# A decoder step on one core: in six key slots ScalarE sums two pages over the heads and VectorE two instead of three

## Chip, core and metric

One NeuronCore of a Trainium2 chip runs the whole program in one launch. The metric is the device time of one execution in microseconds (us). A core has TensorE (PE), VectorE (DVE), ScalarE (ACT), GpSimd (POOL) and SyncE (SP), each with an instruction stream of its own, and they meet only through semaphores. SyncE does no arithmetic here: it issues nearly all transfers.

## What is computed

One layer of a decoder for 256 prompt rows and 8 sample rows of 1024 columns, in float32. Only the sample rows' attention is touched. Each of the 8 samples has 2048 past tokens, which lie in 16 pages of 128 tokens in a key pool and a value pool:

```python
z = x @ w_in                                    # q | k | v | B | C | h
s = jnp.einsum('bthd,bthnd->bthn', q, k_g) / math.sqrt(HEAD_DIM) - slope * dist
p = jax.nn.softmax(where(valid, s, -inf))       # valid: the top 3 blocks of 256 tokens, and the own one
att = jnp.einsum('bthn,bthnd->bthd', p, v_g)
mix = concat([att, gb * conv(gc * h)]) @ w_out
x1 = layer_norm(ALPHA * x + mix)                # then a gated FFN with a convolution, and a second norm
```

A score is the dot product of a key and the query over the 64 columns of each of 8 heads.

## The kernel before

**Key slots.** The 8 x 16 key pages are worked through in 32 slots of four pages (1 MB), numbered j from 0. Slot j uses buffer j % 4 of the tile KV (in the trace also "qk<-KV,qk" for its products). For each slot the pages are multiplied by the sample's broadcast query into one of two product buffers, `prod[:, j % 2]`, and the products are then summed over the 64 columns of each head into the tile T:

- VectorE multiplies all four pages (`multiply`, L939, 128x2048), or three of them (128x1536) in the slots of `POOLED`, where GpSimd multiplies the fourth (`multiply_page`, L560).
- VectorE sums the first three pages (`reduce`, L949, 1536 products to 24 sums), or all four in the slots of `WHOLE`.
- ScalarE sums the fourth page (`sum_products`, L669): eight copies of 64 columns, each followed by a read of the accumulator.

VectorE multiplies slot j + 1 ahead of the sum of slot j. `multiply(j)` writes over the products of slot j - 2, so it waits until these have been summed: always for VectorE's sum (`s_red`), and for ScalarE's (`s_reda`) only where VectorE itself writes the fourth page.

**Other work in the same streams.** The order on each engine is written out by hand. Between about 100 and 126 us TensorE makes the last projection tiles (`z_tile`, L1437) and the prompt attention's transposes and outputs; ScalarE copies them out of PSUM (`z_tile`, L674, into zbuf; `head_transposes`, L704, into hT; `head_out`, L708, into catT). In ScalarE's order slot 19's sum stands after `head_transposes(2)` and ahead of `z_tile(22)`, `kv_rows(5)`, `head_out(0)`, `head_out(1)` and `head_transposes(3)`. GpSimd gates the convolution's four slices with a product each (L590), with two page products among them, and then does the samples' columns in one small product (L591):

```python
for t in range(4):
    if t >= 2:
        multiply_page(18 + t)
    pool.wait_ge(s_ze, 20 + t + 1)
    nc.gpsimd.tensor_tensor(catT[:, 4 + t, 0:NPR], catT[:, 4 + t, 0:NPR], zT[:, 12 + t, 0:NPR], ALU.mult).then_inc(s_cvT, 1)
nc.gpsimd.tensor_tensor(catT[:, 4:8, NPR:R], cus, zT[:, 12:16, NPR:R], ALU.mult).then_inc(s_cvT, 1)
```

TensorE then waits for all five of these (`s_cvT`) ahead of `values(0, 0)`, L1608, the first product of probabilities with values. From there it runs `values` and `mix_tile` (L1632, L1634) in turn. VectorE's `residual(m)` (L1060) follows each mix tile, between the key slots.

**Transfers.** SyncE issues the loads of keys and values in one fixed sequence (`load_keys`, `load_values`; L360 is the line that both issue from). `load_keys` waits for the product of the slot that last used the buffer. `load_values` waits for the product of TensorE that last read its buffer; that is so from the fourth value load on.

Of the kernel before, what the change touches and what calls it, by code (L numbers as in the profile page):

```python
# [16 lines left out]
ACT = mybir.ActivationFunctionType  # L17
# [11 lines left out]
NH, DH = 8, 64  # L29
DA = NH * DH  # L30
# [10 lines left out]
GP = 4  # L41
SLOTS = NPAGE // GP
GD = GP - 1
# [8 lines left out]
NL = FT - E  # L52
WHOLE = (14, 16, 18, 20, 31)
POOLED = (9, 10, 11, 12) + tuple(range(17, 32))
FIRST_SAMPLES = FT - 4
WARM = 14
HOMES = (6, 4, 5, 6, 4, 5, 6, 4, 5) + tuple((0, 4, 1, 5, 2, 3)[v % 6] for v in range(23))
# [2 lines left out]
def build(nc, x_prompt, x_sample, cache_k, cache_v, state_conv, state_ffn_conv, page_table,  # L60
# [13 lines left out]
    with ctx:  # L74
        def sb(name, shape, dt=F32):
            return ctx.enter_context(nc.sbuf_tensor(name, shape, dt))[:]
# [9 lines left out]
        def sem(name):  # L86
            return ctx.enter_context(nc.semaphore(name))
# [44 lines left out]
        T = sb("T", [P, 2, NPAGE + 1, 4 * NH])  # L132
# [41 lines left out]
        prod = qk[:, 1, :].rearrange("p (u n) -> p u n", u=2)  # L174
# [63 lines left out]
        s_kused, s_vused = sem("k_slot_used"), sem("v_slot_used")  # L238
        s_kpool = sem("k_page_used_pool")
# [91 lines left out]
        def act_sums(j):  # L331
            return sum(i not in WHOLE for i in range(j))

        def pool_pages(j):
            return sum(i in POOLED for i in range(j))

# [7 lines left out]
        def _(sp):  # L344
# [43 lines left out]
            def load_keys(b, s, ids):  # L388
                sp.wait_ge(s_kused, b * SLOTS + (s + 1 - SLOTS))
                if b * SLOTS + s - SLOTS in POOLED:  # L390
                    sp.wait_ge(s_kpool, pool_pages(b * SLOTS + (s + 1 - SLOTS)))
# [132 lines left out]
        def _(pool):  # L524
# [91 lines left out]
            def split_f(u, src):  # L616
                pool.wait_ge(s_f, u + 1)
                nc.gpsimd.tensor_copy(fh[:, u, 0:NPR], src).then_inc(s_fh, 1)
                pool.wait_ge(s_fh, u + 1)
                nc.gpsimd.tensor_tensor(fl[:, u, 0:NPR], src, fh[:, u, 0:NPR], ALU.subtract).then_inc(s_fs, 1)  # L620

            def split_samples(first, end):
                pool.wait_ge(s_sf, 1)
                chain(nc.gpsimd.tensor_copy(fh[:, first:end, NPR:R], sf[:, first:end, :]))
                nc.gpsimd.tensor_tensor(fl[:, first:end, NPR:R], sf[:, first:end, :], fh[:, first:end, NPR:R],
                                        ALU.subtract).then_inc(s_fss, 1)
# [4 lines left out]
            for v in range(NL - 1):  # L631
                split_f(E + v, ftmp[:, v % 2, :])
                if v == FIRST_SAMPLES - E:
                    split_samples(0, FIRST_SAMPLES)
            pool.wait_ge(s_var2, 1)
# [8 lines left out]
        def _(act):  # L644
# [14 lines left out]
            def sum_products(j):  # L659
                b, s = divmod(j, SLOTS)  # L660
                if j in WHOLE:
                    return
                if j in POOLED:
                    act.wait_ge(s_kpool, pool_pages(j + 1))
                else:
                    act.wait_ge(s_kused, j + 1)
                for h in range(NH):
                    x = prod[:, j % 2, GD * DA + h * DH:GD * DA + (h + 1) * DH]
                    ins = nc.scalar.activation(x, x, ACT.Copy, accum_out=T[:, b // 4, GP * s + GD, b % 4 * NH + h:b % 4 * NH + h + 1])  # L669
                ins.then_inc(s_reda, 1)  # L670

            def z_tile(n):
# [51 lines left out]
            load_win(1)  # L724
            query(1)
            sum_products(0)
            for j in range(1, 4):
                z_tile(j - 1)
                query(2 * j)
                query(2 * j + 1)  # L730
                sum_products(j)
# [8 lines left out]
            for j in range(4, 8):  # L740
                sum_products(j)
                z_tile(j)
# [88 lines left out]
            def silu(u):  # L831
                act.wait_ge(s_cv, 2 * u + 1)
                nc.scalar.activation(U[:, u % 2, 0, :], U[:, u % 2, 0, :], ACT.Silu).then_inc(s_si, 1)
# [31 lines left out]
            def late_scaled(v):  # L865
                u = E + v
                for a in range(2):
                    act.wait_ge(s_u, 2 * u + a + 1)
                    act.wait_ge(s_f, u - 1)
                    bank = ps[:, 2 * late_slot(v) + a, :]  # L870
                    nc.scalar.activation(U[:, u % 2, a, :], bank[:, 0:NPR], ACT.Copy, scale=tap(u + a * FT, 2))
                    nc.scalar.activation(uptail[:, :, u + a * FT], bank[:, TAIL:R], ACT.Copy).then_inc(s_tl, 1)

            for v in range(NL - 1):
# [6 lines left out]
                if v >= 1:  # L881
                    silu(E + v - 1)
                if v == FIRST_SAMPLES - E + 1:
                    act.wait_ge(s_sv, 1)
                    nc.scalar.activation(sf[:, 0:FIRST_SAMPLES, :], cs2[:, 0:FIRST_SAMPLES, :], ACT.Silu).then_inc(s_si8, 1)
            late_scaled(NL - 1)
# [3 lines left out]
            act.wait_ge(s_sv, 2)  # L890
            nc.scalar.activation(sf[:, FIRST_SAMPLES:FT, :], cs2[:, FIRST_SAMPLES:FT, :], ACT.Silu).then_inc(s_si8, 1)
            act.wait_ge(s_f, FT)
            act.wait_ge(s_sf, 2)
            act.wait_ge(s_fss, 3)
            for c in range(3):
                act.wait_ge(s_utps, c + 1)
                n = min(4, NTAIL - 4 * c)
# [9 lines left out]
        def _(dve):  # L907
# [21 lines left out]
            def multiply(j):  # L929
                b, s = divmod(j, SLOTS)  # L930
                dve.wait_ge(s_qb, b + 1)
                dve.wait_ge(s_kv[s], 16 * GP * b + 16 * GP)
                if j >= 2:
                    dve.wait_ge(s_red, j - 1)
                    if j not in POOLED:
                        dve.wait_ge(s_reda, act_sums(j - 1))
                n = GD if j in POOLED else GP
                q = qb[:, b:b + 1, :].to_broadcast([P, n, DA])
                nc.vector.tensor_tensor(prod[:, j % 2, 0:n * DA].rearrange("p (g d) -> p g d", g=n), kv[:, s, 0:n], q,  # L939
                                        ALU.mult).then_inc(s_kused, 1)  # L940

            def reduce(j):
                b, s = divmod(j, SLOTS)
                n = GP if j in WHOLE else GD
                dve.wait_ge(s_kused, j + 1)
                if j in WHOLE and j in POOLED:
                    dve.wait_ge(s_kpool, pool_pages(j + 1))
                dst = T[:, b // 4, GP * s:GP * s + n, b % 4 * NH:(b % 4 + 1) * NH]
                nc.vector.tensor_reduce(dst, prod[:, j % 2, 0:n * DA].rearrange("p (g h d) -> p g h d", h=NH, d=DH),  # L949
                                        AX.X, ALU.add).then_inc(s_red, 1)  # L950

            def scan(j):
                if j + 1 < NS * SLOTS:
                    multiply(j + 1)
                reduce(j)
# [102 lines left out]
            def residual(m):  # L1058
                dve.wait_ge(s_mix, m + 1)
                nc.vector.scalar_tensor_tensor(rT[:, m, :], xT[:, m, :], ALPHA, ps[:, mix_bank(m), 0:R], ALU.mult, ALU.add)\  # L1060
                    .then_inc(s_r1, 1)

            multiply(0)
            for j in range(8):
                scan(j)
# [24 lines left out]
            scan(15)  # L1090
            head_reciprocals(2)
            multiply(17)
            reduce(16)
            gate_penalties(0)
            head_masked(3)
            multiply(18)
            token_max(0)
            max_diagonal(0)
            reduce(17)
            head_reciprocals(3)  # L1100
            shifted_scores(0)
# [41 lines left out]
            _, x, _, out = first_rows[1]  # L1143
# [113 lines left out]
            for a in range(2):  # L1257
                src = ps[:, 7, :].rearrange("p (n a x) -> p a n x", a=2, x=32)
                ins = nc.vector.tensor_copy(tails[:, a, 0:E, :], src[:, a, 0:E, 0:NS])
            ins.then_inc(s_ett, 1)  # L1260

            def late_convolved(v):
                u, s = E + v, late_slot(v)
                if v < NL - 1:
                    convolved(u, ps[:, 2 * s, 0:NPR], ps[:, 2 * s + 1, 0:NPR])
                    return
                for a in range(2):
                    for k in (1, 0):
                        n = NPR - 2 + k
                        if k:  # L1270
                            dve.wait_ge(s_tl, E + 2 * v + a + 1)
                        else:
                            dve.wait_ge(s_c1, 2 * u + a + 1)
                        out = U[:, u % 2, a, 2 - k:NPR]
                        nc.vector.scalar_tensor_tensor(out, ps[:, 2 * s + a, 0:n], tap(u + a * FT, k), out, ALU.mult, ALU.add)\
                            .then_inc(s_c1 if k else s_cv, 1)
# [17 lines left out]
            for v in range(NL):  # L1294
# [6 lines left out]
                late_convolved(v)  # L1301
                if v == FIRST_SAMPLES - E:
                    dve.wait_ge(s_cst, 1)
# [67 lines left out]
            n, _, _, out = row_tiles[2]  # L1371
# [563 lines left out]
```

## Time and profile before

| what | value |
|---|---|
| median of 3 runs | 438.06 us (437.49 to 438.96) |
| profiled execution | 437.8 us, of which 436.0 us span |
| TensorE busy | 412.7 us, 95% |
| VectorE busy | 294.7 us, 68% |
| ScalarE busy | 181.4 us, 42% |
| GpSimd busy | 110.8 us, 25% |
| moved by DMA | 124.60 MB, mean 286 GB/s |

The span is what the profiler saw between the first and the last instruction; the rest of the 437.8 us lies around it. A share of busy time is a mean over stages with different limits: the key slots end at about 183 us, and from 262 us on the FFN's products keep TensorE busy with little else.

### The profile page before, as it was taken

What the parts mean: (1) busy time and instruction counts of PE and PEld (TensorE: products, weight loads), DVE (VectorE), ACT (ScalarE), POOL (GpSimd) and SP (SyncE); (2) the same over time, 40 slices, a digit from 0 to 9 for tenths busy, and PEclk for the clock granted to TensorE, in tenths of its full rate; (3) what the DMA queues carried; (4) which work ended last, traced back from release to release, by engine and by line L of the source; (5) the groups of instructions that cost most, each with busy time, mean ns of one, the idle gap of its engine ahead of it and who ended that gap; (6) DMA issues with size and microseconds to landing.
All of it is one profiled execution on the core that took longest, in us unless ns stands there. A gap on an engine that the chain in (4) does not pass through costs nothing.

```text
span 436.0 us, 8237 instructions
## 1 busy us (share of the span) xinstructions
PE 412.7 (95%) x2903; PEld 339.2 (78%) x2903; DVE 294.7 (68%) x382; ACT 181.4 (42%) x694; POOL 110.8 (25%) x133
## 2 busy tenths in 40 slices
PE   4999999999999998999999989999999999999990
PEld 4588887876876774765653479999999999999990
DVE  0498999999799976954541275666776776534437
ACT  1587569644469133112110243554455555233201
POOL 1005334995255152200000717122211220000002
PEclk9999999999999999999999999999999999999997
DMA  8999999899999999999999953665556766676002
GB/s 313 397 359 407 405 407 393 316 404 409 409 359 327 338 404 405 406 405 404 402 405 398 318 196 98 194 191 162 158 169 191 213 181 186 183 211 206 3 2 99
DMA packets 109515, 124.60 MB, mean 286 GB/s; under 512 B 5903, under 2 KB 67048, under 8 KB 109466
## 3 DMA queue, kind: packets, MB, share of 16 engines
q1 hardware_dynamic: 101138, 107.30, 70.2%
q10 hardware_dynamic: 8336, 16.78, 10.2%
q8 instruction: 23, 0.38, 0.3%
q14 instruction: 18, 0.15, 0.1%
HBM read 121.65 MB, written 2.61 MB: 285 GB/s over the span
## 4 chain that ended last, share of the span: by engine, by line
PE 64%; DVE 18%; DMA 5%; issue 5%; SPq 4%; POOL 2%; ACT 1%; DVEq 0%; POOLq 0%; ACTq 0%
PE ps L1821 12%; PE ps L1822 11%; PE ps L1823 11%; PE ps L1714 8%; PE ps L1608 6%; DVE qk L939 6%; DVE T L949 5%; PE ps L1437 4%; PE ps L1632 4%; PE ps L1634 3%; PE ps L1384 3%; SPq L360 2%; DMA wring<-in_cache_v 2%; DMA KV<-in_cache_k 2%; POOL x1l L612 1%
## 5 line engine op out<-in xcount | busy, mean ns | idle before, releaser
L1188 DVE TENSOR_TENSOR wlo<-KV,whi 128x2048 fp32r<-128x2048 f32 (+1 forms) x24 | 61.7, 2571 | 57.5 <-ACT whi L838 29.3
L1437 PE MATMUL ps<-xT,wring 128*128 128x264 f32 x384 | 89.6, 388 | 0.1
L1437 PEld LDWEIGHTS ps<-xT,wring 128*128 128x128 f32 x384 | 71.6, 190 | 13.6 <-issue 1.7
L1821 PE MATMUL ps<-x1h,whi 128*128 128x264 f32 x256 | 73.7, 288 | 0.2
L1822 PE MATMUL ps<-x1l,whi 128*128 128x264 f32 x256 | 72.7, 284 | 0.0
L1823 PE MATMUL ps<-x1h,wlo 128*128 128x264 f32 x256 | 72.6, 284 | 0.0
L939 DVE TENSOR_TENSOR qk<-KV,qk 128x1536 f32<-128x1536 f32 (+1 forms) x32 | 67.0, 2097 | 6.6 <-DMA KV<-in_cache_k 2.7
L669 ACT ACTIVATE qk<-qk 128x64 f32<-128x64 f32 x216 | 51.9, 245 | 29.1 <-POOL qk L560 23.1
L949 DVE TENSOR_REDUCE T<-qk 128x24 f32<-128x1536 f32 (+1 forms) x32 | 58.4, 1827 | 0.0
L1821 PE MATMUL ps<-fh,whi 128*128 128x264 f32 x176 | 50.4, 286 | 0.1
L1822 PE MATMUL ps<-fl,whi 128*128 128x264 f32 x176 | 50.0, 284 | 0.0
L1823 PE MATMUL ps<-fh,wlo 128*128 128x264 f32 x176 | 49.9, 284 | 0.0
L1821 PEld LDWEIGHTS ps<-x1h,whi 128*128 128x128 f32 x256 | 48.2, 188 | 1.7 <-issue 1.3
L838 ACT ACTIVATE whi<-KV 128x2048 fp32r<-128x2048 f32 x16 | 30.7, 1916 | 42.4 <-PE ps L1823 42.4
L1822 PEld LDWEIGHTS ps<-x1l,whi 128*128 128x128 f32 x256 | 48.3, 188 | 0.0
L1823 PEld LDWEIGHTS ps<-x1h,wlo 128*128 128x128 f32 x256 | 48.1, 188 | 0.0
L560 POOL TENSOR_TENSOR qk<-KV,qk 128x512 f32<-128x512 f32 x19 | 33.3, 1758 | 37.9 <-DMA KV<-in_cache_k 23.7
L669 ACT ACTIVATION_READ_ACCUMULATOR qk<-qk 128x1 f32 x216 | 41.0, 190 | 0.0
L1168 DVE SCALAR_TENSOR_TENSOR U<-ps,stT,U 128x255 f32<-128x255 f32 (+1 forms) x84 | 34.5, 474 | 0.0
L1821 PEld LDWEIGHTS ps<-fh,whi 128*128 128x128 f32 x176 | 33.2, 188 | 0.6 <-DVE wlo L1188 0.5
L1822 PEld LDWEIGHTS ps<-fl,whi 128*128 128x128 f32 x176 | 33.2, 188 | 0.0
L1823 PEld LDWEIGHTS ps<-fh,wlo 128*128 128x128 f32 x176 | 33.1, 188 | 0.0
(215 smaller groups left out, 574.0 us busy)
## 6 DMA issues: line engine op xcount, KB each, us to landing
KV<-in_cache_k SPq DMA_DIRECT2D x128, 256.0 KB, 6.2
KV<-in_w_ffn_up SPq DMA_DIRECT2D x32, 512.0 KB, 4.7
KV<-in_cache_v SPq DMA_DIRECT2D x60, 256.0 KB, 7.3
wring<-in_cache_v SPq DMA_DIRECT2D x56, 256.0 KB, 6.4
KV<-in_w_ffn_down SPq DMA_DIRECT2D x8, 1408.0 KB, 6.3
wring<-in_w_in ACTq DMA_DIRECT2D x5, 2048.0 KB, 14.0
zbuf<-in_cache_v SPq DMA_DIRECT2D x12, 256.0 KB, 5.3
zbuf<-in_w_ffn_up SPq DMA_DIRECT2D x3, 1024.0 KB, 10.2
```

The costliest lines, as they stand in the source:

```text
L560: nc.gpsimd.tensor_tensor(prod[:, j % 2, GD * DA:GP * DA], kv[:, s, GD, :], qb[:, b, :], ALU.mult).then_inc(s_kpool, 1)
L669: ins = nc.scalar.activation(x, x, ACT.Copy, accum_out=T[:, b // 4, GP * s + GD, b % 4 * NH + h:b % 4 * NH + h + 1])
L838: nc.scalar.activation(whi[s][:, 0:UNIT], w2[s][:, 0:UNIT], ACT.Copy).then_inc(s_hi, 1)
L939: nc.vector.tensor_tensor(prod[:, j % 2, 0:n * DA].rearrange("p (g d) -> p g d", g=n), kv[:, s, 0:n], q, ALU.mult).then_inc(s_kused, 1)
L949: nc.vector.tensor_reduce(dst, prod[:, j % 2, 0:n * DA].rearrange("p (g h d) -> p g h d", h=NH, d=DH), AX.X, ALU.add).then_inc(s_red, 1)
L1168: nc.vector.scalar_tensor_tensor(out, bank[:, 0:n], tap(u + a * FT, k), out, ALU.mult, ALU.add)\
L1188: nc.vector.tensor_tensor(wlo[s][:, 0:n], w2[s][:, 0:n], whi[s][:, 0:n], ALU.subtract).then_inc(s_lo, 1)
L1437: ins = nc.tensor.matmul(ps[:, z_bank(n), 0:R], tile[k], xT[:, k, :], start=k == 0, stop=k == KT - 1)
L1714: ins = nc.tensor.matmul(ps[:, u % 4, a * NPR:(a + 1) * NPR], early(u, k, a), x1T[:, k, 0:NPR], start=k == 0, stop=k == KT - 1)
L1821: nc.tensor.matmul(out, wh[k], xh[k], start=k == 0, stop=False)
L1822: nc.tensor.matmul(out, wh[k], xl[k], start=False, stop=False)
L1823: ins = nc.tensor.matmul(out, wl[k], xh[k], start=False, stop=k == n - 1)
```

## The change

In the six slots of a new table `HALVED`, `reduce` sums two pages on VectorE (1024 products to 16 sums) in place of three. `sum_products` sums the third page as well as the fourth on ScalarE: sixteen copies in place of eight. The third page's part waits for VectorE's product and the fourth's for GpSimd's. Since ScalarE now reads products that VectorE wrote, `multiply(j)` on VectorE waits for ScalarE's sums where slot j - 2 is in the table.

```diff
+HALVED = (17, 19, 22, 24, 26, 28)
...
-                if j in POOLED:
-                    act.wait_ge(s_kpool, pool_pages(j + 1))
-                else:
-                    act.wait_ge(s_kused, j + 1)
-                for h in range(NH):
-                    x = prod[:, j % 2, GD * DA + h * DH:GD * DA + (h + 1) * DH]
-                    ins = nc.scalar.activation(x, x, ACT.Copy, accum_out=T[:, b // 4, GP * s + GD, b % 4 * NH + h:b % 4 * NH + h + 1])
+                for g in range(2 if j in HALVED else GD, GP):
+                    if g == GD and j in POOLED:
+                        act.wait_ge(s_kpool, pool_pages(j + 1))
+                    else:
+                        act.wait_ge(s_kused, j + 1)
+                    for h in range(NH):
+                        x = prod[:, j % 2, g * DA + h * DH:g * DA + (h + 1) * DH]
+                        ins = nc.scalar.activation(x, x, ACT.Copy, accum_out=T[:, b // 4, GP * s + g, b % 4 * NH + h:b % 4 * NH + h + 1])
...
-                    if j not in POOLED:
+                    if j not in POOLED or j - 2 in HALVED:
                         dve.wait_ge(s_reda, act_sums(j - 1))
...
-                n = GP if j in WHOLE else GD
+                n = GP if j in WHOLE else 2 if j in HALVED else GD
```

ScalarE's stream around slot 19's sum, before (hT and hT_53 are the prompt attention's transposes, zbuf the projection, catT the outputs):

```order
L681 ACTIVATE rows<-ps 128x512
L704 ACTIVATE hT<-ps 128x384 x2
L669 ACTIVATE qk,T<-qk 128x64 x8
L674 ACTIVATE zbuf<-ps 128x264
L683 ACTIVATE srows<-ps 8x512
L708 ACTIVATE catT<-ps 128x256 x2
L704 ACTIVATE hT_53<-ps 128x384 x2
L674 ACTIVATE zbuf<-ps 128x264
L708 ACTIVATE catT<-ps 128x256 x2
L803 ACTIVATE ctail<-ps 10x512
```

The same place of the changed kernel, whose lines stand two lower:

```order
L683 ACTIVATE rows<-ps 128x512
L706 ACTIVATE hT<-ps 128x384 x2
L671 ACTIVATE qk,T<-qk 128x64 x16
L676 ACTIVATE zbuf<-ps 128x264
L685 ACTIVATE srows<-ps 8x512
L710 ACTIVATE catT<-ps 128x256 x2
L706 ACTIVATE hT_53<-ps 128x384 x2
L676 ACTIVATE zbuf<-ps 128x264
L710 ACTIVATE catT<-ps 128x256 x2
L805 ACTIVATE ctail<-ps 10x512
```

Eight copies more stand ahead of everything that ScalarE does from `z_tile(22)` on.

VectorE's stream from the product of slot 20 to that of slot 22, before (Pw, ownp and vsT belong to the samples' softmax):

```order
L939 TENSOR_TENSOR qk<-KV,qk 128x1536 [waits scores_summed_dve,k_landed0,q_broadcast]
L949 TENSOR_REDUCE T<-qk 128x3x8 [waits k_slot_used]
L1036 TENSOR_TENSOR ownp<-T,rden 64x4x4 [waits sample_values_copied]
L1038 TENSOR_TENSOR ownp<-ownp,vsT 128x4x4 [waits own_weights]
L939 TENSOR_TENSOR qk<-KV,qk 128x1536 [waits k_landed1,scores_summed_dve,q_broadcast,dve_chain]
L949 TENSOR_REDUCE T<-qk 128x4x8 [waits k_page_used_pool,k_slot_used]
L939 TENSOR_TENSOR qk<-KV,qk 128x1536 [waits scores_summed_dve,k_landed2,q_broadcast]
```

And of the changed kernel:

```order
L941 TENSOR_TENSOR qk<-KV,qk 128x1536 [waits scores_summed_dve,k_landed0,q_broadcast]
L951 TENSOR_REDUCE T<-qk 128x2x8 [waits k_slot_used]
L1038 TENSOR_TENSOR ownp<-T,rden 64x4x4 [waits sample_values_copied]
L1040 TENSOR_TENSOR ownp<-ownp,vsT 128x4x4 [waits own_weights]
L941 TENSOR_TENSOR qk<-KV,qk 128x1536 [waits scores_summed_dve,k_landed1,scores_summed_act,q_broadcast,dve_chain]
L951 TENSOR_REDUCE T<-qk 128x4x8 [waits k_page_used_pool,k_slot_used]
L941 TENSOR_TENSOR qk<-KV,qk 128x1536 [waits scores_summed_dve,k_landed2,q_broadcast]
```

Slot 19's sum is a page shorter, and slot 21's product waits for `scores_summed_act`, which it did not.

## Rows read from the trace of the kernel before

**Rows 1.** Busy time by engine in three stretches, with DMA share and rate

```profile
125.00:150.00 25.00, 24.43 (x136) 16.78 (x132) 24.73 (x18) 15.18 (x115) 10.98 (x8) 1.00 0.95 323
150.00:226.00 76.00, 74.28 (x458) 47.01 (x450) 47.64 (x82) 16.63 (x72) 10.21 (x5) 1.00 1.05 404
226.00:237.00 11.00, 9.67 (x62) 4.93 (x66) 2.08 (x3) 0.00 (x0) 0.00 (x0) 1.00 1.05 403
```

**Rows 2.** Waits of SyncE's queue, 100 to 170 us: total, times, longest

```profile
SPq L360 <- DVE qk L939: 6.8, 3, 3.2
SPq L360 <- PE ps L1608: 2.2, 1, 2.2
```

**Rows 3.** TensorE's timeline: start, us, [idle before <- releaser]

```profile
126.27 0.60 PE L1384 MATMUL ps<-ident,zbuf 128*10 128x128 f32 x4 [0.57 <-ACT catT L708]
126.80 1.06 PE L1608 MATMUL ps<-zbuf,Pw 128*32 128x512 f32 x8
...
226.37 1.07 PE L1608 MATMUL ps<-KV,Pw 128*32 128x512 f32 x8 [0.45 <-DMA KV<-in_cache_v]
...
234.12 1.06 PE L1608 MATMUL ps<-KV,Pw 128*32 128x512 f32 x8 [0.80 <-DMA KV<-in_cache_v]
...
236.70 1.07 PE L1608 MATMUL ps<-wring,Pw 128*32 128x512 f32 x8 [0.17 <-DMA wring<-in_cache_v]
```

**Rows 4.** ScalarE's timeline around the sums of slots 17, 19 and 27

```profile
101.43 0.26 ACT L669 ACTIVATE qk<-qk 128x64 f32<-128x64 f32 x1 [5.75 <-POOL qk L560]
...
119.59 0.26 ACT L669 ACTIVATE qk<-qk 128x64 f32<-128x64 f32 x1
...
121.41 0.19 ACT L669 ACTIVATION_READ_ACCUMULATOR qk<-qk 128x1 f32 x1
121.50 0.37 ACT L674 ACTIVATE zbuf<-ps 128x264 f32<-128x264 f32 x1
...
122.78 0.83 ACT L704 ACTIVATE hT<-ps 128x384 f32<-128x384 f32 x2
...
125.74 0.38 ACT L708 ACTIVATE catT<-ps 128x256 f32<-128x256 f32 x1 [0.27 <-PE ps L1488]
...
147.97 0.26 ACT L669 ACTIVATE qk<-qk 128x64 f32<-128x64 f32 x1 [6.38 <-POOL qk L560]
```

**Rows 5.** VectorE's timeline: slots 19 to 22, and the last residual

```profile
120.02 1.75 DVE L949 TENSOR_REDUCE T<-qk 128x24 f32<-128x1536 f32 x1
...
122.75 2.77 DVE L939 TENSOR_TENSOR qk<-KV,qk 128x1536 f32<-128x1536 f32 x1
125.44 2.27 DVE L949 TENSOR_REDUCE T<-qk 128x32 f32<-128x2048 f32 x1
127.85 1.76 DVE L939 TENSOR_TENSOR qk<-KV,qk 128x1536 f32<-128x1536 f32 x1
...
164.29 0.43 DVE L1060 SCALAR_TENSOR_TENSOR xT<-xT,ps 128x264 f32<-128x264 f32 x1 [2.10 <-PE ps L1634]
```

**Rows 6.** GpSimd's timeline at the same place

```profile
121.95 0.73 POOL L590 TENSOR_TENSOR catT<-catT,zbuf 128x256 f32<-128x256 f32 x1 [5.29 <-ACT zbuf L674]
122.64 1.27 POOL L560 TENSOR_TENSOR qk<-KV,qk 128x512 f32<-128x512 f32 x1
124.70 1.40 POOL L590 TENSOR_TENSOR catT<-catT,zbuf 128x256 f32<-128x256 f32 x1 [0.80 <-ACT zbuf L674]
126.07 0.25 POOL L591 TENSOR_TENSOR catT<-cu,zbuf 128x32 f32<-128x32 f32 x1
```

**Rows 7.** GpSimd's timeline at 262 us

```profile
262.62 0.73 POOL L620 TENSOR_TENSOR fl<-qk,fh 128x256 fp32r<-128x256 f32 x1
263.30 2.46 POOL L618 CAST fh<-qk 128x256 fp32r<-128x256 f32 x1
...
266.52 0.40 POOL L618 CAST fh<-qk 128x256 fp32r<-128x256 f32 x1
```

**Rows 8.** VectorE's timeline at 263 us

```profile
263.08 2.42 DVE L1188 TENSOR_TENSOR wlo<-KV,whi 128x2048 fp32r<-128x2048 f32 x1 [3.53 <-ACT whi L838]
```

## Prediction

> **What bounds the kernel now.** I first cut the span into stretches. From 125 to 150 us VectorE is busy 24.73 of 25 us, and TensorE 24.43; the transfers run at 323 GB/s. From 150 to 226 us they run at 404 GB/s, and at 403 from there to 237 us, which I take as full; TensorE is still busy 74.28 of 76 us [rows 1]. So two things are full at once: TensorE, and later the transfers. Between 125 and 150 us the transfers could have carried a quarter more: 25 us x (1 - 323/404) = 5.0 us of their time is lost there. Whoever gives buffers back sooner in that stretch may shift all that follows.
>
> Who does? In the waits of SyncE's queue, VectorE's product holds it three times for 6.8 us in total, TensorE's `values` once for 2.2 us [rows 2]. VectorE's longest, 3.2 us, is for slot 20's product; in VectorE's order that product stands behind a softmax step which itself waits for a projection tile of TensorE. After 130 us the queue's one wait of any size is that for `values`, since from the fourth value load on a value page can only be fetched when TensorE has read the one before it.
>
> TensorE's timeline shows what it lacks. At 126.27 us it has waited 0.57 us for ScalarE's copy of catT, at 126.80 us `values(0, 0)` begins. At the end of the value loads it waits for transfers three times, 0.45 + 0.80 + 0.17 = 1.42 us [rows 3]. Nothing in between waits for VectorE's key slots: at 164.29 us the last `residual` has itself waited 2.10 us for TensorE [rows 5]. VectorE is full from 125 to 150 us, but is ahead of those who need it.
>
> **What VectorE saves.** A sum of three pages takes 1.75 us, one of four 2.27 us [rows 5], 0.52 us a page. Two pages cost some 1.23 us by that. Six slots save 6 x 0.52 = 3.1 us of VectorE. I cost this at nothing on the path: slot 17's saving goes into waits for ScalarE's exponentials and for TensorE, slot 19's into the wait below, and those of 22 to 28 into the 2.10 us at 164 us and what was ahead of it.
>
> **What ScalarE gets.** Eight copies with their reads took 121.50 - 119.59 = 1.91 us [rows 4]. Six slots add 11.5 us to ScalarE. In most this is hidden: slot 17's fourth page comes after a wait of 5.75 us for GpSimd, slot 27's after 6.38 us [rows 4], and the third page's products are there long before, so that it is summed inside such a wait; the slots around have ones of the same kind or, at 22 and 24, a backlog of one page against a cycle of two slots on VectorE of 8 us. Without that cover each would cost its 1.91 us.
>
> **Slot 19 is different.** Its sum begins at 119.59 us, straight behind `head_transposes(2)`, and ScalarE goes on at 121.50 us without a gap [rows 4]. There is no wait to hide in. All behind it comes 1.91 us later until ScalarE's next idle time. Step by step:
>
> 1. Slot 19's last read ended at 121.41 + 0.19 = 121.60 us and now ends at 123.51. The copy of tile 22 ended at 121.50 + 0.37 = 121.87 and now ends at 123.78.
> 2. `multiply(21)` on VectorE, which began at 122.75 us [rows 5], now waits for slot 19. It begins at about 123.65 us. Before, it took 2.77 us in place of the 1.76 us of slot 22's [rows 5], since GpSimd had begun a product at 122.64 that lasted to 123.91 [rows 6]: it ended 1.61 us after that. Now it is alone and ends at 123.65 + 1.76 = 125.4 us, as before. Queued behind it are VectorE's sum of 20 and the slots after, which so lose nothing.
> 3. GpSimd's gating of slice 2 waits for tile 22 and began at 121.95, 0.08 us after the copy [rows 6]; now at 123.86 us. That is 0.2 us after `multiply(21)` began, and the two don't run at once: the gating at 124.70 us took 1.40 us in place of 0.73, and ended 0.58 us after VectorE's product of 122.75 to 125.52 [rows 5, 6]. So slice 2 ends at 125.4 + 0.6 = 126.0 us, page 21's product (1.27 us) at 127.25, slice 3 (0.73 us) at 127.95.
> 4. VectorE's sum of 20 (2.27 us, which doesn't hinder GpSimd) ends at 127.6, and `multiply(22)` is issued 0.14 us later as before [rows 5], at 127.75 us: while slice 3 is under way, and ahead of GpSimd's last small product, L591. What happens then is seen at 263 us: VectorE's product was issued at 263.08 during a GpSimd product that ended at 263.35; GpSimd's next, issued at 263.30, took 2.46 us in place of 0.40, to 265.76, and VectorE's ended at 265.50 [rows 7, 8]. VectorE goes in between. So `multiply(22)` runs from 127.95 for 1.61 us to 129.55, and L591 ends at about 129.7 us. It ended at 126.07 + 0.25 = 126.32 us [rows 6].
> 5. `values(0, 0)` waits for it. It began at 126.80 us [rows 3] and now begins at 129.75 us: 2.95 us later. By ScalarE's copies alone (its second pair of hT copies ends at 122.78 + 0.83 + 1.91 = 125.5, the last copy of catT moves from 125.74 to about 126.6 us) [rows 4] it would be 0.85 us.
>
> The page "SBUF — State Buffer" of the Trainium skill, section "Who interferes with whom", says that a VectorE instruction with two SBUF inputs and a GpSimd one that reads SBUF exclude each other, that issue order decides, and that `tensor_reduce` never contends; the trace agrees in all three. By it step 4 comes out as written.
>
> **From there to the end.** TensorE has a fixed order and no idle time until 165 us that could take this up. At 226 to 237 us, 1.42 us of waiting for transfers could: if the transfers came no later, TensorE would lose only 2.95 - 1.42 = 1.53 us. But they do come later. SyncE stands at `load_values(4)` until `values(0, 1)` is done [rows 2], the later value loads follow the same rule, and from 150 us on the transfers are full, so a pause of theirs is never made good. With all of it passed on the cost is 2.95 us. The pause need not grow by as much as TensorE's delay, since key loads between are not held by TensorE; I take 2.6 us, nearer the upper bound, as the stretch of 323 GB/s shows that little is queued there. Behind 237 us all follows TensorE at a fixed distance.
>
> Sum: 437.8 - 0 + 2.6 = 440.4 us for the profiled execution. This one lies 0.26 us under the median of the runs shown, so 440.5 us stands between the two. About 0.3%, 1.3 us, is what a measurement of this kernel can tell from no change.
>
> **Rivals.**
>
> - *L591 slips through.* If `multiply(22)` is issued 0.2 us later against GpSimd than I have it, L591 goes first and `values(0, 0)` begins at 128.2 us: 1.4 us late, and 438.8 to 439.4 us at the end. The margin of step 4 is only those 0.2 us, which speaks for it; that L591 is as late if `multiply(22)` comes earlier speaks against it.
> - *Hidden.* The delay at 126.8 us is only the 0.85 us of ScalarE's copies, or the transfers don't shift, and the 1.42 us take up most of it: 437.7 to 438.6 us. For it: a wait of the right size exists. Against it: the gating on GpSimd hangs on the same copy, and the loads on the same `values`.
> - *Faster.* VectorE's 3.1 us give key buffers back sooner, the 5.0 us of lost transfer time shrink, and TensorE's 1.42 us of waiting go: 437.8 - 1.4 = 436.4 us. It decides from where slot 19's extra 1.91 us is hidden and VectorE sets the releases. For it: 24.73 of 25 us busy and 6.8 us of SyncE's waits. Against it: after 130 us SyncE waits for TensorE. More than 1.4 us it can't be, as TensorE's own order is then the bound. The Trainium skill's page "Perfetto Trace Analysis", section "Optimizing Scalar/DVE Operations", speaks for this one: with VectorE saturated, moving work to ScalarE may make sense. The trace has the saturation, at 24.73 of 25 us, but not the dependence on it.
> - *Worse.* GpSimd's later pages push the key loads of 21 and 22 too, and the pause grows past 2.95 us: 441.3 to 443 us.
>
> **How the numbers follow.** Full collision 0.50 (439.6 to 441.3 us), L591 slipping through 0.20, hidden 0.15, faster 0.10, worse 0.05. The time is the first case's. The range from 438.0 to 441.5 us leaves out the faster case, part of the hidden one and the worse one. Slower by over 0.3% begins at 439.4 us: the first, the worst, and some of the second, less what the untested 0.2 us takes from my trust in the first: 0.60. Faster 0.10, the same 0.30. The first case's own range is 439.6 to 441.3 us.
>
> **What would show it.** In the changed kernel's trace ScalarE's copy of tile 22 ends near 123.8 us; `multiply(21)` begins near 123.65 us behind an idle time that ScalarE ended; GpSimd's gating of slice 2 lasts to 126.0 us; L591 ends near 129.7 us (128.2 us for the first rival, below 127 us for the hidden case), and `values(0, 0)` follows it at once. The load behind `values(0, 1)` is 2.95 us later. VectorE's two-page sums take 1.2 us each. The prediction is wrong if L591 isn't the last of the five that TensorE waits for, if SyncE's loads from 137 to 150 us don't move with `values`, or if two-page sums let the key loads at 130 us start sooner.

## The result and the profile after

The changed kernel takes 443.16 us (median of 4 runs, 442.0 to 443.76) against 437.84 us for the kernel before: a ratio of 1.0114, 95% interval 1.009 to 1.0138, or 5.0 us slower by the ratio. The range of the prediction ended at 441.5 us. The direction was right, the size was not.

The profiled execution took 442.0 us with a span of 440.2 us, 4.2 us more than that of the kernel before. Its lines stand two lower (one on GpSimd). Part of it only began later: the first matmul of the softmax gate, which both kernels make behind the same work, starts at 99.67 us before and at 100.31 us after. That start differs from execution to execution: in the two profiles below of the kernel before with one move or one delay it is at 100.46 and 100.06 us, and nothing ahead of it was changed there. TensorE's timeline, of the kernel before:

```profile
99.67 0.49 PE L1511 MATMUL ps<-alibir,identr 128*128 128x512 f32 x1 [0.86 <-DVE penx L998]
...
127.79 2.05 PE L1632 MATMUL ps<-catT,wring 128*128 128x264 f32 x8
...
135.00 1.07 PE L1608 MATMUL ps<-wring,Pw 128*32 128x512 f32 x8
```

and of the changed one, from there on, in which `values(0, 0)` is the product at 130.47 us:

```profile
100.31 0.49 PE L1513 MATMUL ps<-alibir,identr 128*128 128x512 f32 x1 [0.86 <-DVE penx L1000]
...
127.69 0.60 PE L1386 MATMUL ps<-ident,zbuf 128*10 128x128 f32 x4 [0.61 <-ACT catT L710]
130.47 1.94 PE L1610 MATMUL ps<-zbuf,Pw 128*32 128x512 f32 x8 [2.18 <-issue]
132.33 2.77 PE L1634 MATMUL ps<-catT,wring 128*128 128x264 f32 x8
...
140.26 1.07 PE L1610 MATMUL ps<-wring,Pw 128*32 128x512 f32 x8
...
238.29 1.07 PE L1610 MATMUL ps<-KV,Pw 128*32 128x512 f32 x8 [0.53 <-DMA KV<-in_cache_v]
```

I measure everything from that gate matmul. `values(0, 0)` comes 130.47 - 100.31 = 30.16 us behind it, before 126.80 - 99.67 = 27.13 us: 3.03 us later. `values(0, 1)`, at 140.26 us after and at 135.00 us before, comes 39.95 us behind it instead of 35.33: 4.62 us later. So 1.59 us more are lost between two products that have only TensorE's own work between them. `values(0, 0)` takes 1.94 us where it took 1.06 [rows 3], and the product of `mix_tile` behind it 2.77 us where it took 2.05: these two are the whole 1.6 us. At 140.26 us `values` takes 1.07 us again. The windows of the changed kernel show why (the number behind the busy times is the granted clock, then DMA share and GB/s):

```profile
126.00:130.00 4.00, 1.65 (x16) 0.79 (x12) 3.87 (x3) 2.74 (x15) 4.00 (x4) 1.00 0.98 341
130.00:131.00 1.00, 0.53 (x4) 0.23 (x8) 1.00 (x2) 1.00 (x11) 1.00 (x2) 0.71 0.92 326
131.00:132.00 1.00, 1.00 (x8) 0.00 (x0) 0.87 (x2) 1.00 (x10) 1.00 (x2) 0.50 0.93 338
...
133.00:134.00 1.00, 1.00 (x4) 0.79 (x3) 1.00 (x1) 1.00 (x10) 0.00 (x0) 0.59 0.25 78
134.00:135.00 1.00, 1.00 (x6) 0.84 (x6) 1.00 (x2) 1.00 (x10) 0.19 (x1) 1.00 0.94 320
```

The granted clock is 1.00 until 130 us, 0.50 from 131 to beyond 133 us, and 1.00 again from 134 us: TensorE falls from 2.4 to 1.2 GHz at the end of its 2.18 us of idle time.

The first stretch of [rows 1], after. TensorE's busy time from 125 to 150 us is 2.5 us less, part of it spent at the low clock, and the transfers lose more of their time, 275 against 323 GB/s:

```profile
125.00:150.00 25.00, 21.89 (x113) 14.65 (x117) 21.73 (x16) 18.92 (x144) 11.55 (x9) 0.93 0.81 275
```

SyncE's queue, as in [rows 2]: VectorE holds it for 6.7 us as before, TensorE's `values` for 6.9 us where it was 2.2. The largest holder in both lists is GpSimd's page product, 7.1 us before and 7.7 after, which [rows 2] and the prediction leave out.

```profile
SPq L361 <- PE ps L1610: 6.9, 3, 3.8
SPq L361 <- DVE qk L941: 6.7, 3, 3.4
```

ScalarE, as in [rows 4]: slot 17's fourth page still waits for GpSimd (3.69 us in place of 5.75, the rest is now the third page's sum); slot 19's sixteen copies run without a gap from 120.23 us, and tile 22 is copied at 124.05 us.

```profile
102.07 0.26 ACT L671 ACTIVATE qk<-qk 128x64 f32<-128x64 f32 x1 [3.69 <-POOL qk L561]
...
120.23 0.26 ACT L671 ACTIVATE qk<-qk 128x64 f32<-128x64 f32 x1
...
124.05 0.38 ACT L676 ACTIVATE zbuf<-ps 128x264 f32<-128x264 f32 x1
...
127.17 0.38 ACT L710 ACTIVATE catT<-ps 128x256 f32<-128x256 f32 x1 [0.48 <-PE ps L1490]
```

VectorE, as in [rows 5]:

```profile
120.66 1.21 DVE L951 TENSOR_REDUCE T<-qk 128x16 f32<-128x1024 f32 x1
...
124.28 1.76 DVE L941 TENSOR_TENSOR qk<-KV,qk 128x1536 f32<-128x1536 f32 x1 [1.90 <-ACT qk L671]
...
128.37 1.78 DVE L941 TENSOR_TENSOR qk<-KV,qk 128x1536 f32<-128x1536 f32 x1
```

GpSimd, as in [rows 6]. The last row is the samples' small product: 1.76 us in place of 0.25. The first is slice 2, which meets VectorE's product at 124.28 us and takes 2.13 us in place of 0.73.

```profile
124.50 2.13 POOL L591 TENSOR_TENSOR catT<-catT,zbuf 128x256 f32<-128x256 f32 x1 [7.20 <-ACT zbuf L676]
126.59 1.26 POOL L561 TENSOR_TENSOR qk<-KV,qk 128x512 f32<-128x512 f32 x1
127.82 0.71 POOL L591 TENSOR_TENSOR catT<-catT,zbuf 128x256 f32<-128x256 f32 x1
128.50 1.76 POOL L592 TENSOR_TENSOR catT<-cu,zbuf 128x32 f32<-128x32 f32 x1
```

VectorE's sums by form (busy, mean ns): 1744 - 1208 = 536 ns are saved in each of six slots, 3.2 us.

```profile
L951 DVE TENSOR_REDUCE T<-qk 128x24 f32<-128x1536 f32 x21 | 36.6, 1744 | 0.0
...
L951 DVE TENSOR_REDUCE T<-qk 128x16 f32<-128x1024 f32 x6 | 7.2, 1208 | 0.0
```

### The profile page after: what moved, and what is told of

Same layout as the page of the kernel before. It is cut to its first block, busy times and chain, and to the rows that moved or that the text cites. A ratio compares the mean times of both kernels' runs of the same rounds, so it can differ in the third digit from the quotient of the medians.

```text
span 440.2 us, 8338 instructions
## 1 busy us (share of the span) xinstructions
PE 414.5 (94%) x2903; PEld 340.2 (77%) x2903; DVE 290.5 (66%) x382; ACT 192.6 (44%) x790; POOL 111.1 (25%) x133
## 4 chain that ended last, share of the span: by engine, by line
PE 50%; DVE 17%; SPq 11%; issue 10%; DMA 6%; POOL 3%; ACT 2%; DVEq 0%; POOLq 0%; ACTq 0%
PE ps L1823 11%; PE ps L1824 11%; PE ps L1825 11%; SPq L361 9%; DVE qk L941 5%; DVE T L951 5%; PE ps L1716 4%; PE ps L1439 3%; DMA KV<-in_cache_k 3%; PE ps L1610 2%; PE ps L1386 2%; DMA wring<-in_cache_v 2%; POOL x1l L613 1%; PE ps L1802 1%; DVE wlo L1190 1%
## 5 line engine op out<-in xcount | busy, mean ns | idle before, releaser
L941 DVE TENSOR_TENSOR qk<-KV,qk 128x1536 f32<-128x1536 f32 (+1 forms) x32 | 66.0, 2065 | 11.1 <-DMA KV<-in_cache_k 4.3
L671 ACT ACTIVATE qk<-qk 128x64 f32<-128x64 f32 x264 | 63.3, 244 | 22.6 <-DVE qk L941 13.1
L951 DVE TENSOR_REDUCE T<-qk 128x24 f32<-128x1536 f32 (+2 forms) x32 | 55.2, 1727 | 0.0
L671 ACT ACTIVATION_READ_ACCUMULATOR qk<-qk 128x1 f32 x264 | 50.1, 190 | 0.0
L561 POOL TENSOR_TENSOR qk<-KV,qk 128x512 f32<-128x512 f32 x19 | 31.5, 1660 | 37.9 <-ACT qk L671 18.4
L845 ACT ACTIVATE whi<-KV 128x2816 fp32r<-128x2816 f32 x8 | 20.5, 2558 | 29.8 <-PE ps L1825 29.8
```

Source lines behind the costliest of these rows:

```text
L561: nc.gpsimd.tensor_tensor(prod[:, j % 2, GD * DA:GP * DA], kv[:, s, GD, :], qb[:, b, :], ALU.mult).then_inc(s_kpool, 1)
```

## The experiments

Theory A: slot 19 alone does the harm. Its extra ScalarE work makes GpSimd's small product collide with VectorE's product of slot 22, TensorE waits for it, and its clock drops around that wait. Theory B, the rival: more ScalarE work and VectorE's new waits cost something in every slot.

"Late" below is how much later than in the kernel before `values(0, 0)` and `values(0, 1)` come behind the gate's first matmul, in the profile. The difference in us is the ratio less one, times 437.5 us.

| kernel | late, (0, 0) and (0, 1) | median us | ratio and interval | difference |
|---|---|---|---|---|
| changed kernel | 3.03, 4.62 | 443.16 | 1.0114 (1.009 to 1.0138) | 5.0 |
| without slot 19 | -0.02, -0.01 | 437.56 | 1.0003 (0.999 to 1.0015) | 0.1 |
| slot 19 alone | 3.03, 4.68 | 442.78 | 1.0119 (1.0099 to 1.0138) | 5.2 |
| page 21 last | 0.80, 0.81 | 438.16 | 1.0014 (1.0004 to 1.0024) | 0.6 |
| two idle matmuls | 2.87, 2.87 | 440.32 | 1.0064 (1.0045 to 1.0084) | 2.8 |
| sum 19 early | -0.01, 0.00 | 437.84 | 0.9996 (0.9986 to 1.0006) | -0.2 |
| before, sum 19 early | -0.01, -0.01 | 437.30 | 0.9996 (0.9984 to 1.0008) | -0.2 |
| before, ScalarE delayed | 1.71, 1.72 | 439.16 | 1.0034 (1.0021 to 1.0046) | 1.5 |
| slot 22 waits | 1.51, 1.51 | 439.14 | 1.0031 (1.0019 to 1.0043) | 1.4 |
| one idle matmul | 2.87, 2.88 | 440.78 | 1.0083 (1.007 to 1.0096) | 3.6 |
| changed kernel again | 3.03, 5.95 | 442.65 | 1.0114 (1.0097 to 1.013) | 5.0 |

**Which slots.** One run leaves slot 19 out of the table, the other keeps only it.

```diff
-HALVED = (17, 19, 22, 24, 26, 28)
+HALVED = (17, 22, 24, 26, 28)
```

> The table without slot 19: (17, 22, 24, 26, 28). Theory A (slot 19's extra 1.91 us of ScalarE is the whole cause: it makes GpSimd's small product L592 miss VectorE's product of slot 22, TensorE idles 2.2 us and then works for a while at the lower clock): within 0.5 us of the kernel before, 437.4 to 438.4 us, granted clock 1.00 from 125 to 150 us, values(0, 0) at about 126.8 us after the start of the span. Theory B (the extra ScalarE work and VectorE's new waits in all six slots each cost a share): five sixths of the loss stays, 441.5 to 442.5 us.

```diff
-HALVED = (17, 19, 22, 24, 26, 28)
+HALVED = (19,)
```

> The table with slot 19 alone. Theory A: the whole loss, 442 to 443.5 us. Theory B: one sixth of it, 438.3 to 439.2 us.

Without slot 19 the time is that of the kernel before, to 0.15%; with it alone the whole loss is there. Theory B falls. It also shows that the five other slots bring nothing: 2.7 us less work for VectorE, 9.6 us more for ScalarE, no change in the time.

The profile with slot 19 alone shows the fall of the clock a third time:

```profile
130.65 1.70 PE L1610 MATMUL ps<-zbuf,Pw 128*32 128x512 f32 x8 [2.18 <-issue]
```

```profile
130.00:131.00 1.00, 0.35 (x4) 0.19 (x8) 1.00 (x2) 1.00 (x9) 1.00 (x2) 0.97 0.86 320
131.00:132.00 1.00, 1.00 (x8) 0.00 (x0) 0.99 (x1) 0.30 (x3) 1.00 (x2) 0.50 1.03 231
```

The mean of 0.97 from 130 to 131 us puts the fall at about 130.94 us, some 0.3 us after `values(0, 0)` began and so just behind the idle time of 2.18 us, not in it.

**The collision.** GpSimd's page 21 is moved behind the gating:

```diff
-                if t >= 2:
-                    multiply_page(18 + t)
+                if t == 2:
+                    multiply_page(20)
...
+            multiply_page(21)
             multiply_page(22)
```

> The changed kernel, with GpSimd's product of page 21 moved behind the gating of slice 3 and the samples' product. Theory A: these two are done near 127.6 us, before VectorE's product of slot 22 is issued; TensorE waits only for ScalarE's copies and starts values(0, 0) about 1.0 us later than in the kernel before instead of 3.0; no fall of the granted clock: 438.5 to 439.3 us. If the collision with slot 22's product were not what holds the last product, it would stay at 442 to 443.5 us.

GpSimd's and TensorE's timelines of this run:

```profile
124.71 2.81 POOL L591 TENSOR_TENSOR catT<-catT,zbuf 128x256 f32<-128x256 f32 x2 [7.22 <-ACT zbuf L677]
127.48 0.25 POOL L592 TENSOR_TENSOR catT<-cu,zbuf 128x32 f32<-128x32 f32 x1
```

```profile
128.44 1.06 PE L1611 MATMUL ps<-zbuf,Pw 128*32 128x512 f32 x8
```

Slices 2 and 3 run in turn, the small product takes its 0.25 us again, and `values(0, 0)` is 0.80 us late. It follows the product before it without a wait, so this is ScalarE's copies alone. The run was expected 1.0 us late and at 438.5 us or more; it is a little faster. The other way round, GpSimd's order is kept and VectorE's product of slot 22 is made to wait:

```diff
                 dve.wait_ge(s_kv[s], 16 * GP * b + 16 * GP)
+                if j == 22:
+                    dve.wait_ge(s_cvT, 5)
                 if j >= 2:
```

> The changed kernel, with VectorE's product of slot 22 made to wait for the convolution's five products, so that GpSimd's last small product cannot be shut out. It takes 0.3 us of VectorE. Theory A: L592 takes 0.25 us in place of 1.76, values(0, 0) comes 1.5 us sooner than in the changed kernel, TensorE idles 0.6 us, the granted clock stays at 1.00: 439.0 to 440.0 us. If GpSimd's last product is slow for another reason: 442 to 443.5 us as without it.

```profile
127.92 0.72 POOL L591 TENSOR_TENSOR catT<-catT,zbuf 128x256 f32<-128x256 f32 x1
128.60 0.24 POOL L592 TENSOR_TENSOR catT<-cu,zbuf 128x32 f32<-128x32 f32 x1
```

```profile
129.05 1.06 PE L1612 MATMUL ps<-zbuf,Pw 128*32 128x512 f32 x8 [0.65 <-issue]
```

Only VectorE's product is out of the way, and the small product is back at 0.24 us. So the collision is shown from both sides, and it costs 1.5 us of the 3.0. The small product still ends at 128.84 us, shortly ahead of `values(0, 0)`: 0.7 us of the 1.51 are GpSimd's own, beyond the 0.80 of the copies.

**Delay or new wait.** Here the kernel before gets the delay on ScalarE and nothing of the rest:

```diff
             sum_products(19)
+            spare = ftmp.rearrange("p u n -> p (u n)")
+            sums = stats.rearrange("p r c s -> p (r c s)")
+            for h in range(NH):
+                nc.scalar.activation(spare[:, h * DH:(h + 1) * DH], slope[:, h:h + 1].to_broadcast([P, DH]), ACT.Copy,
+                                     accum_out=sums[:, h:h + 1])
```

> The kernel before, all its sums as they were, with eight copies of 128x64 with accumulator behind slot 19's sum that nobody needs. It gives ScalarE's delay of 1.91 us alone, without VectorE's new wait for slot 19: its product of slot 21 starts at 122.8 us and not at 123.7. Theory A: the collision happens all the same, 0.9 us sooner: L591 ends near 128.8 us, values(0, 0) is 2.0 us late, TensorE idles 1.1 us; 439.3 to 440.0 us if the granted clock holds, 441 to 441.7 us if it falls. If the new wait were the cause: within 0.5 us of the kernel before.

GpSimd's, VectorE's and TensorE's timelines:

```profile
124.24 0.79 POOL L590 TENSOR_TENSOR catT<-catT,zbuf 128x256 f32<-128x256 f32 x1 [7.21 <-ACT zbuf L674]
...
126.25 0.72 POOL L590 TENSOR_TENSOR catT<-catT,zbuf 128x256 f32<-128x256 f32 x1
126.93 1.76 POOL L591 TENSOR_TENSOR catT<-cu,zbuf 128x32 f32<-128x32 f32 x1
```

```profile
122.69 1.76 DVE L944 TENSOR_TENSOR qk<-KV,qk 128x1536 f32<-128x1536 f32 x1
...
126.77 1.81 DVE L944 TENSOR_TENSOR qk<-KV,qk 128x1536 f32<-128x1536 f32 x1
```

```profile
128.90 1.06 PE L1613 MATMUL ps<-zbuf,Pw 128*32 128x512 f32 x8 [0.86 <-issue]
```

The product of slot 21 starts unhindered at 122.69 us, that of slot 22 at 126.77 us, again while slice 3 is under way, and the small product is shut out for 1.76 us just the same. ScalarE's delay is enough for this collision. It gives 1.71 us of the 3.03. The other 1.3 us are a second collision: here slice 2 takes 0.79 us, in the changed kernel 2.13, as VectorE's product of slot 21 has waited for ScalarE there and starts just ahead of it. All of GpSimd's work behind slice 2 comes 1.34 us later by that. The shares of the two collisions depend on which is taken away first (1.5 and 0.7 us, or 0.9 and 1.3), as TensorE waits for whichever of the small product and the catT copies ends last. The run was expected at 2.0 us late and 439.3 us or more, and came out a little under both. The granted clock is 1.00 throughout 125 to 150 us here.

**The clock.** TensorE gets something to do while it waits: `keep_clock(5, 512)` is a matmul of 512 columns whose result nobody reads. None of the work that TensorE waits for comes sooner by that.

```diff
+            pe.wait_ge(s_soft, 1)
+            keep_clock(5, 512)
+            keep_clock(5, 512)
             pe.wait_ge(s_cvT, 5)
```

> The changed kernel, with two idle matmuls of 128x512 on TensorE (about 1 us each) ahead of the wait for the convolution's products, into the 2.2 us in which it idles. Nothing else is sooner. Theory A: the granted clock stays at 1.00, values(0, 0) is as late as in the changed kernel, and the 1.6 us that the low clock took from 130 to 134 us come back: 441.0 to 441.8 us. If the clock's fall does not come from the idle time, or costs nothing: 442.5 to 443.5 us as without it.

```profile
128.28 1.88 PE L1652 MATMUL ps<-ident 128*128 128x512 f32 x4
130.47 1.06 PE L1610 MATMUL ps<-zbuf,Pw 128*32 128x512 f32 x8 [0.30 <-POOL catT L592]
```

`values(0, 0)` is nearly as late as in the changed kernel (2.87 us against 3.03), but takes 1.06 us, and `values(0, 1)` is no later than it: the 1.6 us don't arise. The difference to the kernel before shrinks from 5.0 to 2.8 us, by 2.2 us and not by the 1.6 us of the first profile; the run is faster than the 441.0 us at which its expectation began. Two more runs bear on that. One takes a single `keep_clock` in place of two:

> The changed kernel with one idle matmul of 128x512 (1 us) ahead of the wait in place of two, so that TensorE idles about 1.2 us there. Theory A with the clock falling only for the whole idle time of 2.2 us: as with two, 440.0 to 440.8 us, granted clock 1.00 from 125 to 150 us. If any idle time above about a microsecond at this place drops the clock: 442 to 443.3 us.

```profile
127.99 1.02 PE L1652 MATMUL ps<-ident 128*128 128x512 f32 x2
130.18 1.06 PE L1610 MATMUL ps<-zbuf,Pw 128*32 128x512 f32 x8 [1.17 <-POOL catT L592]
```

TensorE idles 1.17 us, `values(0, 0)` takes 1.06 us and is no later than with two. The run is 0.8 us slower than that one, but the two intervals overlap. Nothing points to a fall of the clock in its other executions: their mean granted clocks are 0.991 to 0.994, and those of the kernel before 0.990 to 0.994. The other run is the changed kernel itself:

> The changed kernel once more, for a second profile and more times beside those of the kernel before on one chip. Theory A: values(0, 0) 3.0 us later after the gate's penalties than before (30.2 against 27.1 us), the granted clock at 0.50 for some 3 us behind it, 442.3 to 443.3 us. If the 5.3 us between the medians had more than these two parts (3.0 and 1.6 us), this profile would show where.

TensorE's timeline and the windows of this second profile, whose execution took 444.51 us:

```profile
100.00 0.49 PE L1513 MATMUL ps<-alibir,identr 128*128 128x512 f32 x1 [0.86 <-DVE penx L1000]
130.16 1.93 PE L1610 MATMUL ps<-zbuf,Pw 128*32 128x512 f32 x8 [2.17 <-issue]
141.28 1.06 PE L1610 MATMUL ps<-wring,Pw 128*32 128x512 f32 x8
```

```profile
126.00:130.00 4.00, 1.39 (x12) 0.71 (x12) 3.87 (x3) 2.75 (x17) 4.00 (x5) 0.92 0.94 318
...
135.00:136.00 1.00, 1.00 (x4) 0.79 (x3) 0.16 (x1) 1.00 (x10) 0.79 (x1) 0.50 0.91 330
136.00:137.00 1.00, 1.00 (x5) 0.83 (x5) 0.00 (x0) 0.26 (x3) 0.57 (x1) 0.91 0.97 318
```

`values(0, 0)` is 3.03 us late again (30.16 us behind the gate matmul), `values(0, 1)` 5.95 us (41.28 us). The clock fell earlier within the same idle time and stayed at 0.50 until past 136 us instead of to beyond 133 us: it costs 5.95 - 3.03 = 2.9 us here and 1.6 us in the first profile. The 2.2 us by medians lie between the two, and the executions of this run spread from 441.08 to 444.51 us. The spread goes with the clock: over the ten executions of the changed kernel the two lowest mean granted clocks, 0.983 and 0.985, belong to the two slowest, 443.76 and 444.51 us, and the highest, 0.993, to the fastest, 441.08 us. That one's mean is like those of the kernel before, which suggests that its clock did not fall, and it takes about what the executions with one idle matmul take, 440.3 to 441.26 us.

**A place where ScalarE has time.** ScalarE waits for TensorE ahead of the copies of `head_transposes(2)`. Slot 19's sum goes in there, in the changed kernel:

```diff
             kv_rows(3)
+            sum_products(19)
             head_transposes(2)
-            sum_products(19)
             z_tile(22)
```

> The changed kernel, with slot 19's sum on ScalarE moved ahead of head_transposes(2), into the 5 us in which ScalarE waits there for TensorE. All sixteen copies (3.8 us) fit. Theory A: nothing is late any more, all six slots' savings on VectorE stay, and the time is that of the kernel before or a little less: 437.0 to 438.0 us. Theory B (extra ScalarE work costs wherever it is): 441 to 443 us.

The other run makes the same move in the kernel before, where the sum has one page.

> The kernel before, with the same move of slot 19's sum and nothing else. It shows what the move alone is worth: ScalarE's copies for TensorE come up to 1.9 us sooner, of which TensorE can use at most the 0.57 us that it waited for catT. Both theories: 437.0 to 437.9 us. If this and the run with the changed kernel agree, the two-page sums are worth nothing.

ScalarE's and TensorE's timelines and the window of 125 to 150 us, of the first of these:

```profile
120.05 0.87 ACT L706 ACTIVATE hT<-ps 128x384 f32<-128x384 f32 x2 [1.24 <-PE ps L1490]
120.81 0.40 ACT L676 ACTIVATE zbuf<-ps 128x264 f32<-128x264 f32 x1
```

```profile
127.48 0.60 PE L1386 MATMUL ps<-ident,zbuf 128*10 128x128 f32 x4 [0.57 <-ACT catT L710]
128.01 1.06 PE L1610 MATMUL ps<-zbuf,Pw 128*32 128x512 f32 x8
```

```profile
125.00:150.00 25.00, 24.43 (x134) 16.99 (x133) 24.72 (x20) 19.71 (x153) 12.56 (x8) 1.00 0.98 340
```

ScalarE sums both pages and still has 1.24 us of waiting left, tile 22 is copied at once behind the hT copies, and nothing is late. The whole loss is gone with all six slots in place, so it was a matter of where slot 19's sum stood. But there is no gain either: 0.9996, as for the kernel before with the same move. TensorE waits the same 0.57 us for catT and is busy 24.43 of 25 us as in [rows 1], although the transfers run at 340 instead of 323 GB/s. No version tried is measurably faster than the kernel before.

## Why the prediction was right or wrong

Times of the changed kernel are given here less 0.64 us, its later start.

**Right: steps 1 to 5.** The copy of tile 22 ended at 124.05 + 0.38 - 0.64 = 123.79 us (123.78 forecast). `multiply(21)` began at 123.64 us and ended at 125.40 (123.65, 125.4). Slice 2 ended at 125.99 us, slice 3 at 127.89 (126.0, 127.95). `multiply(22)` began at 127.73 us (issued at 127.75), the small product, L592 now, ended at 129.62 (129.7), and `values(0, 0)` was 3.03 us late (2.95). ScalarE's copies alone make 0.80 us of it, as the run with page 21 last shows (0.85 forecast), the collision 1.5 us, as slot 22's wait shows from the other side, and slice 2's collision with `multiply(21)`, which is step 3, the other 0.7 (worked out from these runs; no run takes it away alone). The Trainium skill's page "SBUF — State Buffer" says in its section "Who interferes with whom" that a VectorE instruction with two SBUF inputs contends with a GpSimd instruction that reads SBUF. These runs agree: moving either engine's product took the 1.76 us back to 0.25 or 0.24.

**Right: VectorE's saving is worth nothing, and so are ScalarE's five other slots.** The two-page sums saved 3.2 us (3.1 forecast). Without slot 19 the ratio is 1.0003, and with slot 19 at no cost 0.9996.

**Wrong: "From there to the end".** This step priced TensorE's wait as a delay and nothing else. Its sentence that TensorE "has a fixed order and no idle time until 165 us that could take this up" is true, but TensorE worked slower behind this wait. The term that is missing, put at nothing without a reason, is the clock: 1.6 us more were lost before `values(0, 1)` in one profile and 2.9 us in the other, 0.9 us of either in `values(0, 0)`, which took 1.94 and 1.93 us for 1.06. With the wait filled, the loss of the medians goes from 5.0 to 2.8 us. That leaves 440.32 us, where the forecast, which had no clock in it, stood at 440.5.

**Off in size: the passing-on.** The same step took 2.6 of 2.95 us as reaching the end, since key loads need not follow TensorE. The runs in which the clock stays up say how much does: 0.80 us late gave 0.6 us, 1.51 gave 1.4, 1.71 gave 1.5 and 2.87 gave 2.8 with two idle matmuls and 3.6 with one, to 0.4 to 0.6 us either way by their intervals, the 2.8 to 0.9. Nearly all of it passes on, as the upper bound had it; why the 3.6 lies above its 2.87 is not shown. SyncE issued the value load behind `values(0, 1)` at 141.53 us in place of 136.26, 4.6 us later from the gate, as late as that product: the loads do follow `values`. In [rows 3] the 1.42 us of waiting for transfers looked like a place to make up time. The changed kernel's profile has 0.53 us of it left, but that wait is not a fixed store: the runs that are not late at all have 0.71 us (without slot 19), 0.18 and 0.18 us (slot 19's sum early, in either kernel) there, and by the medians it made up little at most.

**The rivals.** "L591 slips through" did not happen in the changed kernel. The run in which slot 22 waits is that case, 1.51 us late where the rival had 1.4, and 1.4 us slower. "Hidden" and "faster" fell; for the latter, VectorE holds SyncE's queue for 6.7 us as before, and taking slot 19's cost away brought no 1.4 us. "Worse" had about the right size of time (to 443 us) by another mechanism: it wanted key loads that push the pause beyond 2.95 us, and what came was the clock.

**Open.** Why the clock fell at about 130.4 us in one profile (1.00 until 130, 0.71 in the next us) and at about 129.4 in the other (0.92 from 126 to 130), and stayed low for some 3 and some 7 us, is not settled; nor is whether the 0.8 us between one and two idle matmuls are real.

## What to carry to other kernels

Extra work for an engine that has spare time is free only if it is put into one of that engine's waits; look at what stands directly behind the new work, and move it ahead of the wait if it isn't needed later. Where a small operation of GpSimd releases another engine, see which product VectorE issues while the operation before it runs: a delay far upstream can bring the two together. Price a new wait of TensorE of some 2 us, as here, twice, once as a delay and once at the lower clock behind it, and before taking work off a full engine ask who waits for it.

## What the runs showed of the hardware

The granted clock fell to 0.50 within an idle time of TensorE of 2.18 or 2.17 us in both profiles of the changed kernel, and some 0.3 us behind one of 2.18 us in the profile with slot 19 alone. It stayed at 1.00 behind waits of 1.17, 0.86, 0.65 and 0.30 us in the runs above. How long it stayed low differed between executions of the same program, some 3 us in one and some 7 in the other.

VectorE's product that was issued while a GpSimd product ran went in between that and GpSimd's next, even though the two stood back to back in GpSimd's order. The next then took 1.76 us in place of 0.25, in the changed kernel and in the one with the delay alone, and 2.46 us in place of 0.40 in [rows 7].
